# Turning normalized rows with scaled diagonal products, and letting the next product start block by block

## The chip, the cores and the metric

The kernel runs on one core of a Trainium2 chip. The metric is the device time of one execution of the whole program in microseconds (us). PE is TensorE, DVE VectorE, ACT ScalarE, POOL GpSimd and SP the engine whose queue issues the weight loads.

## The reference, cut to what matters

The reference is a small network: two layers of a first model, then one of a second, on 256 tokens (`SEQ`) of width 1024 (`D`), all in float32. Between the large parts stand norms over the width:

```python
def layer_norm(x, g, b):
    mu = jnp.mean(xf, axis=-1, keepdims=True)
    var = jnp.mean(jnp.square(xf - mu), axis=-1, keepdims=True)
    y = (xf - mu) * lax.rsqrt(var + LN_EPS) * g + b
...
h = rmsnorm(x, norm1_g) * (1.0 + sc1) + sh1      # second model, before its mixer
h2 = rmsnorm(x, norm2_g) * (1.0 + sc2) + sh2     # before its mixture of experts
return rmsnorm(x, final_norm_g)
```

The order is: mixer (attention and a state-space scan), norm, mixture of experts, norm, mLSTM mixer, norm, mixture, norm; then rms norm, three-branch mixer, rms norm, mixture with 32 experts, and the last rms norm.

## The kernel before, in words

The stream of tokens lies in `net.x` as two row tiles (i = 0, 1) of 128 tokens by 1024. Products want the tokens along the free axis, so each norm also makes `net.xT`, eight blocks (k = 0 to 7) of 128 features by 256 tokens. A phase is a class with one method per engine; each engine runs through the list `PHASES` in order, so the order on an engine is the order of the code, and engines meet at semaphores. DVE, ACT and POOL wait for each of their own instructions before the next (`Steps`, L71).

Seven norms lie in the list. ln0 and ln2 stand before the first two mixtures, ln1 before the mLSTM mixer, ln3 directly before rms0 (with nothing between), rms1 before the third mixture, and rms2 at the end. A turned norm (`LayerNorm` L389, `RmsNorm` L1489) runs like this for a row tile:

- DVE adds the last product to x (L496, L2779, L2368) and takes statistics (L401, L403, L404), or ACT sums squares (L1540, L1551) and DVE forms the mean (L1509, L1513, L1514).
- POOL raises the variance to the power -0.5 (L467, L1609).
- DVE writes the normalized rows, 128 by 1024, to scratch `xn` (L414, L1522).
- PE turns the eight blocks into two PSUM banks, four in each, by `pe.transpose` (L439, L1590).
- ACT evicts the first bank, blocks 0 to 3 (L478, L1563), and DVE the second, blocks 4 to 7 (L457, L1602), with the norm's gain and offset as per-partition scalars.

PE then waits until all four banks of the two row tiles are free (`wait_freed`, L114, called at L441 and L1592) before it goes on to the next phase's first product. That is the router's logits in a mixture (L2498), the gate strips in mLSTM and in the three-branch mixer (`small_strips`, L263). In the mixtures the scratch rows `xn` are also used later: `self.src` (L2455) is the same memory, and L2528 gathers tokens out of it. Between the logits and the gather lie one ACT copy (L2850), a fold on PE (L2505), zero products that open the output banks (L2509), and a chain of small DVE operations that picks experts and slots (L2696 to L2735).

ln3 is different: it isn't turned. DVE makes the finished rows in place (`finish`, L423 and L425, 128 by 1024 each), ACT squares the whole row (L1540), and rms0 normalizes and turns those.

POOL clears three buffers of a mixture (L2801, L2803) directly after the second `pow` of the norm before it. Before rms0 PE makes a row of gates (L1476); before the second row tile of rms1 it makes the strips for another (L1456).

## Time and profile before

| | us |
|---|---|
| median of 3 runs (1987.6 to 1993.73) | 1990.02 |
| the profiled execution, whole | 1990.63 |
| its span, first to last instruction | 1988.7 |
| PE busy | 1805.1 (91%) |
| DVE busy | 576.9 (29%) |
| ACT busy | 354.3 (18%) |
| POOL busy | 209.1 (11%) |

The rest of the page is an average over stages. The norms are short stretches in which PE isn't full; they are read from the timeline and the chain of waits. TensorE's granted clock is given as a share of its high level (2.4 GHz): 1.00 is the high and 0.50 the low level of 1.2 GHz. A float32 product stands as two MATMUL instructions; a transpose stands as one.

### The profile page before, as it was taken

The page shows a single profiled execution, that of the slowest core. Times are in us where ns is not written, and L with a number is a line of the kernel's source. Part 1 is how long each engine was busy: PE and PEld are TensorE (multiplying, and loading weights), DVE is VectorE, ACT ScalarE, POOL GpSimd, SP SyncE. Part 2 cuts the span into 40 slices and gives each one's busy share as a digit, 9 for nine tenths or more (in the row PEclk, how much of TensorE's full clock was granted, in tenths as well). Part 3 has the DMA queues.
Part 4 walks back from the last instruction along what each step waited for, and adds up shares of the span by engine and source line. Part 5 has one row for each costly group of instructions (what it writes and reads, how often), then busy time and mean ns, then how long its engine had stood idle before and what let it go on. Part 6 is the DMA issues. An engine that isn't in the chain of part 4 may idle for free.

```text
span 1988.7 us, 21335 instructions
## 1 busy us (share of the span) xinstructions
PE 1805.1 (91%) x6924; PEld 942.6 (47%) x6925; DVE 576.9 (29%) x1242; ACT 354.3 (18%) x654; POOL 209.1 (11%) x347
## 2 busy tenths in 40 slices
PE   8888699799978998999989999999988998888886
PEld 7444333485733336855865476444443333333332
DVE  8882400487641013321263321001131000000002
ACT  1242211212312112022141100112022111101101
POOL 0551122000002210000000000000001101101100
PEclk9868899898989998999999999999989999999999
DMA  9003399657325994323412334432255999999995
GB/s 367 22 1 146 138 382 397 248 222 285 145 110 229 393 397 188 140 116 136 180 75 95 148 136 160 162 133 95 121 239 206 422 422 422 422 422 422 422 422 237
DMA packets 70438, 468.81 MB, mean 236 GB/s; under 512 B 7848, under 2 KB 12112, under 8 KB 15072
## 3 DMA queue, kind: packets, MB, share of 16 engines
q1 hardware_dynamic: 66016, 457.56, 57.0%
q10 hardware_dynamic: 4352, 10.35, 1.5%
q8 instruction: 40, 0.66, 0.1%
q14 instruction: 30, 0.25, 0.0%
HBM read 466.82 MB, written 1.06 MB: 235 GB/s over the span
## 4 chain that ended last, share of the span: by engine, by line
PE 62%; DVE 16%; DMA 15%; issue 3%; ACT 2%; ACTq 1%; POOL 0%; SPq 0%; DVEq 0%; POOLq 0%
PE bank L238 17%; DMA ring_sb<-stream 15%; PE bank L2630 11%; PE bank L251 10%; PE bank L1628 4%; PE bank L2646 4%; PE bank L2670 4%; PE bank L2528 2%; DVE scratch_sb L1136 2%; DVE scratch_sb L1331 2%; DVE scratch_sb L997 2%; PE bank L916 1%; PE bank L1900 1%; PE bank L1272 1%; DVE scratch_sb L1419 1%
## 5 line engine op out<-in xcount | busy, mean ns | idle before, releaser
L2630 PE MATMUL bank<-ring_sb,scratch_sb 128*64 128x512 f32 x1536 | 344.2, 595 | 53.3 <-DMA ring_sb<-stream 29.3
L251 PE MATMUL bank<-xT_sb,ring_sb 128*128 128x256 f32 x1216 | 265.4, 381 | 0.0
L2630 PEld LDWEIGHTS bank<-ring_sb,scratch_sb 128*64 128x64 f32 x1536 | 116.8, 137 | 280.5 <-issue 280.5
L251 PEld LDWEIGHTS bank<-xT_sb,ring_sb 128*128 128x128 f32 x1216 | 231.5, 191 | 34.3 <-issue 2.9
L2670 PE MATMUL bank<-ring_sb,scratch_sb 128*64 128x512 f32 x768 | 171.9, 596 | 10.5 <-ACT scratch_sb L2889 10.5
L238 PE MATMUL bank<-ring_sb,xT_sb 128*128 128x512 f32 x416 | 179.3, 592 | 0.0
L238 PE MATMUL bank<-ring_sb,scratch_sb 128*128 128x512 f32 x384 | 170.5, 606 | 7.0 <-ACTq L2264 3.6
L2791 DVE TENSOR_TENSOR scratch_sb<-scratch_sb,bank 128x256 f32<-128x256 f32 (+1 forms) x32 | 17.7, 554 | 410.8 <-PE bank L2630 272.1
L238 PEld LDWEIGHTS bank<-ring_sb,xT_sb 128*128 128x128 f32 x416 | 79.0, 190 | 98.2 <-issue 98.1
L238 PEld LDWEIGHTS bank<-ring_sb,scratch_sb 128*128 128x128 f32 x384 | 74.2, 194 | 100.1 <-issue 92.0
L2646 PE MATMUL bank<-scratch_sb 128*128 128x512 f32 x256 | 118.4, 605 | 0.0
L2889 ACT ACTIVATE scratch_sb<-bank 128x256 f32<-128x256 f32 (+1 forms) x96 | 45.4, 490 | 400.9 <-PE bank L2654 255.1
L2796 DVE COPY scratch_sb<-bank 128x512 f32<-128x512 f32 x32 | 22.1, 692 | 300.3 <-PE bank L2670 300.3
L2670 PEld LDWEIGHTS bank<-ring_sb,scratch_sb 128*64 128x64 f32 x768 | 59.3, 137 | 101.3 <-issue 101.3
L2832 POOL COPY scratch_sb<-scratch_sb 128x512 f32 x64 | 37.3, 612 | 569.7 <-PEq L2549 537.0
L1628 PE MATMUL bank<-ring_sb,xT_sb 128*128 128x512 f32 x192 | 84.5, 592 | 0.0
L2646 PEld LDWEIGHTS bank<-scratch_sb 128*128 128x128 f32 x256 | 46.0, 189 | 71.9 <-issue 71.9
L2839 POOL TENSOR_SCALAR scratch_sb<-iota_sb,scratch_sb 128x64 f32<-128x64 f32 x128 | 72.1, 581 | 0.2
L1628 PEld LDWEIGHTS bank<-ring_sb,xT_sb 128*128 128x128 f32 x192 | 36.3, 190 | 42.0 <-issue 41.6
L2528 PE MATMUL bank<-scratch_sb 128*128 128x512 f32 x96 | 46.1, 639 | 10.9 <-DVEq L2737 10.8
L2892 ACT ACTIVATE scratch_sb<-bank 128x256 f32<-128x256 f32 (+1 forms) x32 | 15.7, 491 | 203.3 <-PE bank L2630 203.3
L1331 DVE SCALAR_TENSOR_TENSOR scratch_sb<-ring_sb,mod_sb,scratch_sb 128x512 f32<-128x512 f32 x56 | 42.1, 752 | 2.9 <-DVE scratch_sb L637 0.2
(405 smaller groups left out, 1738.1 us busy)
## 6 DMA issues: line engine op xcount, KB each, us to landing
ring_sb<-stream SPq DMA_DIRECT2D x432, 1024.0 KB, 10.3
rows_sb<-rows ACTq DMA_DIRECT2D x12, 512.0 KB, 4.7
xT_sb<-xT SPq DMA_DIRECT2D x2, 512.0 KB, 7.3
x_sb<-x SPq DMA_DIRECT2D x1, 1024.0 KB, 19.9
scratch_sb<-bias_by_distance ACTq DMA_DIRECT2D x1, 1024.0 KB, 5.2
out<-x_sb ACTq DMA_DIRECT2D x2, 512.0 KB, 2.6
scratch_sb<-decay ACTq DMA_DIRECT2D x1, 768.0 KB, 5.2
small_sb<-small SPq DMA_DIRECT2D x1, 640.0 KB, 13.6
```

Source lines behind the costliest of these rows:

```text
L238: mm = pe.matmul(t[:, :], actT[:, k, i * P:(i + 1) * P], w[:, k % 4, :], start=k == 0, stop=k == kt - 1)
L251: mm = pe.matmul(t[:, m * SEQ:(m + 1) * SEQ], w[:, k % 4, n0:n0 + P], actT[:, k, :], start=k == 0, stop=k == kt - 1)
L997: tt = lambda o, a, b, op: s(dve.tensor_tensor(o, a, b, op))
L1136: self.net.dv(dve.tensor_tensor_scan(xs, self.w[:, 3, j:j + 1].to_broadcast([P, SEQ]), xs, 0.0, ALU.mult, ALU.add))
L1331: net.dv(dve.scalar_tensor_tensor(part, w[:, k, :], c, part, ALU.mult, ALU.add))
L1628: mm = pe.matmul(self.gate_bank[:, :], net.xT[:, kk, i * P:(i + 1) * P], w[:, k, :], start=kk == 0, stop=kk == KT - 1)
L2528: mm = pe.matmul(t[:, :], self.src[:, i, k * P:(k + 1) * P], self.pick[i], start=i == 0, stop=i == 1)
L2630: mm = pe.matmul(t[e * TILE:(e + 1) * TILE, :], self.xs[e][:, kk, :], ws[e][:, k, :], start=kk == 0, stop=kk == KT - 1, skip_group_check=True)
L2646: pe.matmul(T.bank[2 * i + c][:, :], self.scatter[:, i * P:(i + 1) * P], self.y[:, c * 512:(c + 1) * 512], start=False, stop=False, skip_g ...
L2670: mm = pe.matmul(T.bank[6 + c][e * TILE:(e + 1) * TILE, :], self.hidT[:, ff, e * TILE:(e + 1) * TILE], ws[e][:, f, c * 512:(c + 1) * 512], ...
L2839: pool.tensor_scalar(self.weigh[:, i, e * TILE:(e + 1) * TILE], self.net.iota[:, tile * TILE:(tile + 1) * TILE], self.of_pair[:, 0, i, e:e ...
L2889: act.activation(out, src, ACT.Copy).then_inc(self.tile_sem(f"freed{b}", over), 1)
```

## The change

- **Layer norms ln0, ln1, ln2.** DVE no longer writes normalized rows. It writes two diagonals of 128 by 128 per row tile: minus the mean times the reciprocal deviation, and the reciprocal deviation. PE opens a bank with a product of ones and the first diagonal, spread four times over 512 columns, and adds on top of it, block by block, the product of x with the second diagonal. One small DVE operation is added to the statistics, and one after the diagonals.
- **rms0 and rms1.** One diagonal, one product a block, no ones product. The division by the width moves into the scale of ACT's square, and the two DVE operations of the mean become one. The same holds for the mean of rms2.
- **Waits.** `wait_freed` goes. Each eviction counts up a semaphore (`turned_low` by ACT, `turned_high` by DVE), and the next product waits before each of its eight blocks (`await_xT`). Evictions run in the order 0, 2, 1, 3 (0, 1, 2, 3 in rms1).
- **Rows for the gather.** ACT writes the normalized rows after the logits copy (`keep_rows`, two activations of 128 by 1024), and the gather waits for a second count of `logits_kept`.
- **ln3 and rms0.** The finish goes in halves of 512, ACT squares half rows, and row tile 0 gets its diagonal before row tile 1 is finished. The copies of the gate rows on ACT come after the evictions.
- Two semaphores of the mixers become shared with a base; one wait on `c_ready` goes.

```diff
+    def expect_xT(self, low):
+
+        order = {"low": low, "high": [k + 4 for k in low]}
+        for half, ks in order.items():
+            for pos, k in enumerate(ks):
+                self.xT_waits[k] = (self.sem(f"turned_{half}"), 8 * self.n_norms + 4 + pos + 1)
+        self.n_norms += 1
+        return self.n_norms - 1
+
+    def await_xT(self, pe, k):
+
+        if k in self.xT_waits:
+            sem, value = self.xT_waits.pop(k)
+            pe.wait_ge(sem, value)
...
@@ -403,24 +416,47 @@
             s(dve.bn_aggr(st[:, 32 + 4 * i:34 + 4 * i], st[:, 16 * i:16 * i + 12]))
             s(dve.tensor_scalar(st[:, 34 + 4 * i:35 + 4 * i], st[:, 33 + 4 * i:34 + 4 * i], LN_EPS, None, ALU.add))
             dve.sem_inc(self.s("var"), 1)
+            if self.n < 3:
+                s(dve.tensor_scalar(st[:, 50 + i:51 + i], st[:, 32 + 4 * i:33 + 4 * i], -1.0, None, ALU.mult))
 
...
-        else:
-            dve.wait_ge(self.s("rstd"), self.base("rstd") + i + 1)
-            s(dve.tensor_scalar(self.xn[:, i, :], net.x[:, i, :], st[:, 32 + 4 * i:33 + 4 * i],
-                                st[:, 35 + 4 * i:36 + 4 * i], ALU.subtract, ALU.mult))
+            self.scaled_only(dve, i)
+            self.finish_halves(dve, i)
+            return
+        dve.wait_ge(self.s("rstd"), self.base("rstd") + i + 1)
+        rstd, minus = st[:, 35 + 4 * i:36 + 4 * i], st[:, 50 + i:51 + i]
+        s(dve.tensor_scalar(self.diag[:, 2 * i, :], net.ident[:, :], minus, rstd, ALU.mult, ALU.mult))
+        s(dve.tensor_scalar(self.diag[:, 2 * i + 1, :], net.ident[:, :], rstd, None, ALU.mult))
         dve.sem_inc(self.s("normed"), 1)
-
-    def finish(self, dve, i):
+        s(dve.tensor_tensor(st[:, 52 + i:53 + i], minus, rstd, ALU.mult))
...
         for i in range(NT):
             pe.wait_ge(self.s("normed"), self.base("normed") + i + 1)
+            shift = self.diag[:, 2 * i, :].unsqueeze(1).to_broadcast([P, 4, P])
             for c in range(2):
                 t = net.T.open(pe, (self.tag, i, c))
+                pe.matmul(t[:, :].rearrange("p (k t) -> p k t", k=4), net.ones[:, 0:P], shift, start=True, stop=False,
+                          skip_group_check=True)
                 for k in range(4):
                     n0 = (4 * c + k) * P
-                    mm = pe.transpose(t[:, k * P:(k + 1) * P], self.xn[:, i, n0:n0 + P], net.ident[:, :])
+                    mm = pe.matmul(t[:, k * P:(k + 1) * P], net.x[:, i, n0:n0 + P], self.diag[:, 2 * i + 1, :],
+                                   start=False, stop=True, skip_group_check=True)
                 net.T.close((self.tag, i, c), mm)
-        net.T.wait_freed(pe, [(self.tag, i, c) for i in range(NT) for c in range(2)])
+        self.index = net.expect_xT(self.low)
...
     def vector(self, dve):
         net, s = self.net, self.net.dv
+        if self.n == 3:
+            self.following.mean(dve, 0)
+            self.scaled_only(dve, 1)
+            self.following.normalize(dve, 0)
+            self.finish_halves(dve, 1)
+            return
         self.normalize(dve, 1)
-        for i in range(NT if self.n < 3 else 0):
+        for i in range(NT):
             net.T.take(dve, (self.tag, i, 1))
-            for j in range(4, 8):
-                out, t, g, b = self.turned(i, 1, j)
+            for j in self.low:
+                out, t, g, b = self.turned(i, 1, 4 + j)
                 s(dve.tensor_scalar(out, t, g, b, ALU.mult, ALU.add))
+                dve.sem_inc(net.sem("turned_high"), 1)
             net.T.free(dve, (self.tag, i, 1))
...
         for i in range(NT):
             net.T.take(act, (self.tag, i, 0))
-            for j in range(4):
+            for j in self.low:
                 out, t, g, b = self.turned(i, 0, j)
                 net.ac(act.activation(out, t, ACT.Identity, scale=g, bias=b))
+                act.sem_inc(net.sem("turned_low"), 1)
             net.T.free(act, (self.tag, i, 0))
+
+    def keep_rows(self, act, out):
+
+        net, st = self.net, self.net.stat
+        net.T.take(act, (self.tag, NT - 1, 1))
+        act.wait_ge(net.sem("turned_high"), 8 * self.index + 1)
+        for i in range(NT):
+            net.ac(act.activation(out[:, i, :], net.x[:, i, :], ACT.Identity, scale=st[:, 35 + 4 * i:36 + 4 * i],
+                                  bias=st[:, 52 + i:53 + i]))
...
-        self.junk = Arena(net.scratch, JUNK).take(D)
+        self.shared = {"rms": {"mean": NT, "rstd": NT, "normed": NT, "squares": 2 * NT,
+                               "chunk_ready": 2 * NT if n else 0}}
+        self.diag = Arena(net.scratch, NORMED).take(NT * P, NT, P)
+        self.junk = Arena(net.scratch, JUNK).take(512)
         self.strips = Arena(net.scratch, JUNK + D).take(D)
+        self.low = ((0, 2, 1, 3), (0, 1, 2, 3), ())[n]
...
+    def mean(self, dve, i):
+
+        net, st = self.net, self.net.stat
+        dve.wait_ge(self.s("squares"), self.base("squares") + self.squares_at(i, 1))
+        a = 40 + 2 * i
+        net.dv(dve.tensor_scalar(st[:, 2 + i:3 + i], st[:, a:a + 1], st[:, a + 1:a + 2], RMS_EPS, ALU.add, ALU.add))
+        dve.sem_inc(self.s("mean"), 1)
+
     def normalize(self, dve, i):
         net, s, st = self.net, self.net.dv, self.net.stat
-        if self.n == 0:
-            dve.wait_ge(self.s("squares"), self.base("squares") + i + 1)
-            s(dve.tensor_scalar(st[:, 2 + i:3 + i], st[:, i:i + 1], 1.0 / D, RMS_EPS, ALU.mult, ALU.add))
-        else:
-            dve.wait_ge(self.s("squares"), self.base("squares") + self.squares_at(i, 1))
-            a = 40 + 2 * i
-            s(dve.tensor_tensor(st[:, i:i + 1], st[:, a:a + 1], st[:, a + 1:a + 2], ALU.add))
-            s(dve.tensor_scalar(st[:, 2 + i:3 + i], st[:, i:i + 1], 1.0 / D, RMS_EPS, ALU.mult, ALU.add))
-        dve.sem_inc(self.s("mean"), 1)
+        if self.n:
+            self.mean(dve, i)
         dve.wait_ge(self.s("rstd"), self.base("rstd") + i + 1)
         if self.n == 2:
             self.rows_here(dve)
             s(dve.scalar_tensor_tensor(net.x[:, i, :], net.x[:, i, :], st[:, 4 + i:5 + i], net.rows[:, 1, :], ALU.mult,
                                        ALU.mult))
         else:
-            s(dve.tensor_scalar(self.xn[:, i, :], net.x[:, i, :], st[:, 4 + i:5 + i], None, ALU.mult))
+            s(dve.tensor_scalar(self.diag[:, i, :], net.ident[:, :], st[:, 4 + i:5 + i], None, ALU.mult))
         dve.sem_inc(self.s("normed"), 1)
 
...
+        for n, (i, c) in enumerate(self.chunks()):
+            if self.n == 0:
+                act.wait_ge(ln.s("normed"), ln.base("normed") + n + 1)
+            else:
+                act.wait_ge(self.s("chunk_ready"), self.base("chunk_ready") + n + 1)
+            a = 40 + 2 * i + c
+            s(act.activation(self.junk, net.x[:, i, c * 512:(c + 1) * 512], ACT.Square, scale=D ** -0.5,
+                             accum_out=st[:, a:a + 1]))
+            act.sem_inc(self.s("squares"), 1)
...
                 t = net.T.open(pe, (self.tag, i, c))
                 for k in range(4):
                     n0 = (4 * c + k) * P
-                    mm = pe.transpose(t[:, k * P:(k + 1) * P], self.xn[:, i, n0:n0 + P], net.ident[:, :])
+                    mm = pe.matmul(t[:, k * P:(k + 1) * P], net.x[:, i, n0:n0 + P], self.diag[:, i, :], start=True,
+                                   stop=True)
                 net.T.close((self.tag, i, c), mm)
-        net.T.wait_freed(pe, [(self.tag, i, c) for i in range(NT) for c in range(2)])
+        self.index = net.expect_xT(self.low)
 
     def vector(self, dve):
         net, s = self.net, self.net.dv
-        for i in range(self.n > 0, NT):
-            self.normalize(dve, i)
-        for i in range(NT if self.n < 2 else 0):
+        if self.n == 2:
+            self.normalize(dve, 1)
+            return
+        if self.n == 1:
+            self.normalize(dve, 1)
+        for i in range(NT):
             net.T.take(dve, (self.tag, i, 1))
-            for j in range(4, 8):
-                out, t, scale, bias = self.turned(i, 1, j)
+            for j in self.low:
+                out, t, scale, bias = self.turned(i, 1, 4 + j)
                 s(dve.tensor_scalar(out, t, scale, bias, ALU.mult, ALU.add))
+                dve.sem_inc(net.sem("turned_high"), 1)
+                if (self.n, i, j) == (0, 0, 2):
+                    self.mean(dve, 1)
             net.T.free(dve, (self.tag, i, 1))
+            if (self.n, i) == (0, 0):
+                self.normalize(dve, 1)
...
+
+    def keep_rows(self, act, out):
+
+        net, st = self.net, self.net.stat
+        net.T.take(act, (self.tag, NT - 1, 1))
+        for i in range(NT):
+            net.ac(act.activation(out[:, i, :], net.x[:, i, :], ACT.Copy, scale=st[:, 4 + i:5 + i]))
...
         for j in range(per):
             for m in range(strips):
                 k = m * per + j
+                net.await_xT(pe, k)
                 mm = pe.matmul(t[m * width:(m + 1) * width, 0:SEQ], net.small[:, k, at:at + width], net.xT[:, k, :],
                                start=j == 0, stop=j == per - 1, skip_group_check=True)
...
+        pe.wait_ge(self.s("logits_kept"), base("logits_kept") + 2)
         pe.wait_ge(self.s("slots_ready"), base("slots_ready") + 1)
...
         t = T.take(act, (self.tag, "logits"))
         s(act.activation(self.logitsT, t[:, 0:SEQ], ACT.Copy))
         T.free(act, (self.tag, "logits"))
+        act.sem_inc(self.s("logits_kept"), 1)
+        self.prior.keep_rows(act, self.src)
         act.sem_inc(self.s("logits_kept"), 1)
```

In `small_strips` a line `self.await_xT(pe, k)` stands before each matmul as well, and `finish_halves` is the second operation of `finish` (L425) in two halves, each followed by a count of `normed`.

## Rows read from the trace of the kernel before

**Rows 1.** The page, chain that ended last, by engine: share of the span.

```profile
PE 62%; DVE 16%; DMA 15%; issue 3%; ACT 2%; ACTq 1%; POOL 0%; SPq 0%; DVEq 0%; POOLq 0%
```

**Rows 2.** Chain of waits in order of time, ln0: start us, us, what.

```profile
201.78 2.44 DVE scratch_sb L414
204.32 1.98 PE bank L439 x8
...
208.40 1.97 PE bank L2498 x16
210.39 0.39 ACT scratch_sb L2850
```

**Rows 3.** Timeline, ln0, POOL and DVE: start, us, engine, line, operation [idle before].

```profile
198.09 0.81 DVE L414 TENSOR_SCALAR scratch_sb<-x_sb,stat_sb 128x1024 f32<-128x1024 f32 x1 [0.78 <-POOLq L468]
...
201.85 1.81 POOL L2801 MEMSET scratch_sb<- 128x2048 f32 x1 [0.15 <-POOL stat_sb L467]
203.72 1.38 POOL L2803 MEMSET scratch_sb<- 128x1024 f32 x1
204.36 1.75 DVE L457 TENSOR_SCALAR xT_sb<-bank,cols_sb 128x128 f32<-128x128 f32 x4 [0.15 <-DVE scratch_sb L414]
```

**Rows 4.** Groups by line and shape: busy us, mean ns of one | idle before.

```profile
L637 DVE TENSOR_SCALAR scratch_sb<-scratch_sb 128x128 f32<-128x128 f32 x16 | 4.6, 286 | 0.6
L1540 ACT ACTIVATE scratch_sb<-x_sb 128x1024 f32<-128x1024 f32 x2 | 2.1, 1056 | 5.0 <-DVEq L416 5.0
```

**Rows 5.** Timeline of PE, dense stretches of one shape each.

```profile
185.64 13.04 PE L916 MATMUL bank<-ring_sb,scratch_sb 128*128 128x512 f32 x30
...
570.35 1.04 PE L439 MATMUL bank<-ident_sb,scratch_sb 128*128 128x128 f32 x8
...
1000.57 3.81 PE L1879 MATMUL bank<-scratch_sb 128*128 128x128 f32 x32 [0.85 <-issue]
```

**Rows 6.** Stretches of 1 us: length, PE busy (count), PEclk, DMA share, GB/s.

```profile
202.00:203.00 1.00, 0.00 (x0) 0.86 0.95 393
...
376.00:377.00 1.00, 1.00 (x8) 0.90 0.47 197
...
390.00:391.00 1.00, 1.00 (x5) 0.78 0.00 0
...
759.00:760.00 1.00, 0.41 (x3) 0.96 0.02 8
...
1475.00:1476.00 1.00, 0.00 (x0) 0.94 1.08 459
```

**Rows 7.** Timeline, ln1 and the start of mLSTM.

```profile
375.92 1.17 PE L439 MATMUL bank<-ident_sb,scratch_sb 128*128 128x128 f32 x8 [3.61 <-DVEq L416]
...
385.67 0.38 ACT L270 ACTIVATE scratch_sb<-bank 128x256 f32<-128x256 f32 x1 [2.65 <-PE bank L263]
```

**Rows 8.** Timeline, ln3 and rms0.

```profile
749.05 0.69 DVE L2779 SCALAR_TENSOR_TENSOR x_sb<-x_sb,bank 128x512 f32<-128x512 f32 x1 [0.15 <-DVE x_sb L425]
...
755.80 3.61 PE L1590 MATMUL bank<-ident_sb,scratch_sb 128*128 128x128 f32 x16 [4.76 <-DVEq L1523]
...
761.76 1.27 PE L263 MATMUL bank<-xT_sb,small_sb 128*32 128x256 f32 x16 [2.35 <-DVEq L111]
```

**Rows 9.** Timeline, rms1 to the logits of the third mixture.

```profile
1468.20 3.64 PE L1456 MATMUL bank<-ring_sb,mod_sb 128*32 128x512 f32 x32
...
1470.96 2.42 DVE L1522 TENSOR_SCALAR scratch_sb<-x_sb,stat_sb 128x1024 f32<-128x1024 f32 x1 [0.77 <-POOLq L1610]
...
1473.49 1.09 PE L1590 MATMUL bank<-ident_sb,scratch_sb 128*128 128x128 f32 x8 [1.66 <-DVEq L1523]
...
1477.49 3.68 PE L2498 MATMUL bank<-xT_sb,small_sb 128*64 128x256 f32 x16 [2.90 <-DVEq L111]
```

**Rows 10.** Timeline, ACT before the exponentials, and the mean of rms2.

```profile
217.71 0.30 ACT L2855 ACTIVATE scratch_sb<-scratch_sb 128x4 f32<-128x4 f32 x1 [5.48 <-DVEq L2719]
...
1983.19 0.16 DVE L1513 TENSOR_TENSOR stat_sb<-stat_sb 128x1 f32<-128x1 f32 x1 [0.99 <-ACTq L1553]
```

More of the change, by code:

```diff
@@ L111, in free @@
         eng.sem_inc(self.freed[self.jobs[key][0]], 1)
-    def wait_freed(self, eng, keys):
-        for b, k in (self.jobs[key] for key in keys):
-            eng.wait_ge(self.freed[b], k + 1)
 class Arena:
@@ L391 @@
     joins = False
-    shared = {"ln": {"var": NT, "rstd": NT, "normed": NT, "finished": 1}}
+    low = (0, 2, 1, 3)
     def __init__(self, net, n):
         self.net, self.n, self.tag = net, n, f"ln{n}"
-        self.xn = Arena(net.scratch, NORMED).take(NT * D, NT, D)
+        self.shared = {"ln": {"var": NT, "rstd": NT, "normed": NT if n < 3 else 2 * NT, "finished": 1}}
+        self.diag = Arena(net.scratch, NORMED).take(2 * NT * P, 2 * NT, P)
     def take_chunk(self, dve, i, c):
@@ L423, in finish, with finish_halves @@
         s(dve.scalar_tensor_tensor(x, x, st[:, 32 + 4 * i:33 + 4 * i], net.rows[:, 0, :], ALU.subtract, ALU.mult))
+    def finish_halves(self, dve, i):
+        net, s, st = self.net, self.net.dv, self.net.stat
+        dve.wait_ge(self.s("rstd"), self.base("rstd") + i + 1)
+        for c in range(2):
+            x = net.x[:, i, 512 * c:512 * c + 512]
+            s(dve.scalar_tensor_tensor(x, x, st[:, 35 + 4 * i:36 + 4 * i], net.rows[:, 1, 512 * c:512 * c + 512],
+                                       ALU.mult, ALU.add))
+            dve.sem_inc(self.s("normed"), 1)
+        if i == NT - 1:
+            dve.sem_inc(self.s("finished"), 1)
+    def finish(self, dve, i):
+        net, s, st = self.net, self.net.dv, self.net.stat
+        x = net.x[:, i, :]
+        self.scaled_only(dve, i)
         dve.wait_ge(self.s("rstd"), self.base("rstd") + i + 1)
@@ L698 @@
     tag = "fox"
-    shared = {"head": HEAD_COUNTS}
+    shared = {"head": HEAD_COUNTS, "forget": {"f_ready": 1, "log_ready": 1}}
     INPUT, STATE, REST = (0, 1), (2, 3), (4, 5, 6, 7)
@@ L1171 @@
     tag = "mlstm"
-    shared = {"head": HEAD_COUNTS}
+    shared = {"head": HEAD_COUNTS, "forget": {"f_ready": 1, "log_ready": 1}}
     mlstm = True
@@ L1534, in scalar @@
         net, s, st = self.net, self.net.ac, self.net.stat
+        ln = self.prior
         if self.n == 0:
[L1536 removed]
             keep_gate_strips(net, act, "gt1", self.strips)
[L1538 to L1548 removed]
+        for n, (i, c) in enumerate(self.chunks()):
+            if self.n == 0:
+                act.wait_ge(ln.s("normed"), ln.base("normed") + n + 1)
+            else:
                 act.wait_ge(self.s("chunk_ready"), self.base("chunk_ready") + n + 1)
[L1550 to L1553 removed]
+            a = 40 + 2 * i + c
+            s(act.activation(self.junk, net.x[:, i, c * 512:(c + 1) * 512], ACT.Square, scale=D ** -0.5,
+                             accum_out=st[:, a:a + 1]))
+            act.sem_inc(self.s("squares"), 1)
         if self.n == 2:
@@ L1560, in scalar @@
             net.T.take(act, (self.tag, i, 0))
-            for j in range(4):
+            for j in self.low:
                 out, t, scale, bias = self.turned(i, 0, j)
                 s(act.activation(out, t, ACT.Identity, scale=scale, bias=bias))
+                act.sem_inc(net.sem("turned_low"), 1)
             net.T.free(act, (self.tag, i, 0))
@@ L1566, in scalar @@
                 keep_gate_strips(net, act, "gt2", self.following.gt)
+        if self.n == 0:
+            act.wait_ge(ln.s("finished"), ln.base("finished") + 1)
+            for c in range(2):
+                t = net.T.take(act, ("gt1", c))
+                s(act.activation(net.rows[:, 1, c * 512:(c + 1) * 512], t[:, :], ACT.Copy, scale=1.0 / 32))
+                net.T.free(act, ("gt1", c))
     def turned(self, i, c, j):
```

34 lines of the change are left out of this document (7 added, 27 removed).

## The prediction

> **What bounds the kernel now.** I read the chain that ended last first [rows 1]: PE holds 62% of it, DVE 16%, DMA 15%. So over most of the span a norm matters only by how long it keeps PE from its next product, and I read each norm in the chain of waits and then in the timeline. In ln0 [rows 2] the chain runs from POOL to DVE's normalized rows at 201.78, to the second row tile's transposes at 204.32, through DVE's evictions, to the logits at 208.40, and to ACT at 210.39. The reader is to see that nothing else runs beside it: from PE's start on row tile 1 to ACT's copy it is 6.07 us. ln2 has the same pattern, 376 us later. The 1 us stretches [rows 6] show what PE's clock does there: it fell to the low level at 202.9, after a burst of 1.1 us and a pause, at 376.9 in the burst after a pause, and at 1475.9.
>
> A shift of PE's start behind a norm passes on to the end whole, in either direction: the products behind it keep PE full. In the third mixture, where DMA paces, I take the same, since the loads had stopped before the first expert started and restart with PE; the bound if not is a loss of the rms1 gain below.
>
> **Prices.** A 128x512 float32 product costs 13.04/30 x 2 = 0.87 us at the high level; a 128x128 one 3.81/32 x 2 = 0.24; a transpose 1.04/8 = 0.13 [rows 5]. At the low level I double them: eight transposes took 1.97 there [rows 2] against 1.04. So a row tile of a layer norm goes from 1.04 to 2 x (0.87 + 4 x 0.24) = 3.65 us (low: 1.97 to 7.3), and one of an rms norm to 8 x 0.24 = 1.9 (low 3.8).
> A diagonal on DVE: the same operation and size takes 0.29 [rows 4], about 0.35 for the one with two scalars. The pair with its gap is 0.67, against 0.81 for the full rows [rows 3]. Where no other engine interferes this gives back 0.14, less 0.2 for the small operation behind it.
> An eviction paces at 1.75/4 = 0.45 [rows 3].
> The waits removed: before, DVE's last eviction ended at 204.36 + 2 x 1.75 + 0.2 = 208.1 [rows 3], and ACT's copy came at 210.39, 2.3 us later. After, only the last block's product stays, about a quarter of 1.97 with its start: 0.6. So from row tile 1's start to ACT's copy it is 3.65 + 4 x 0.45 + 0.6 = 6.05 with the clock high, 9.7 low, against 6.07. **The ones product and the dearer turns eat up all of the block-by-block start even at the high clock.**
>
> **POOL's memsets.** In ln0 L414 took 2.44 [rows 2] where the first took 0.81 [rows 3]: the memset of 2048 columns lay beside it, and L414 ended 0.54 after it. So DVE stood still until 203.66. The same is in ln2 and in rms1 (2.42, [rows 9]). A diagonal stands still as well: the first of a pair is done at 203.75; by then the second memset (1.38, of which some 0.5 was its own wait) is next and the second diagonal comes at about 204.7. PE starts at 204.85 instead of 204.32, +0.55. Other end: the diagonals slip in before the memset, PE is ready when row tile 0 is done, 198.85 + 3.65 = 202.5: -1.8. I take +0.55, as all three cases in the trace stood still.
> The Trainium skill, SBUF — State Buffer, "Who interferes with whom", says that whoever issues first gets the shared ports for the whole instruction. In the trace DVE's operation is stamped 0.07 us before the memset [rows 2, 3] and lost all the same, so here the trace speaks against the rule; by the rule the sum would be 2 x 2.35 us lower.
>
> **ln0 and ln2.** Before, PE began row tile 0 at 198.09 + 0.81 + 0.1 = 199.0 [rows 3] and paused from 200.1 to 204.32, 4.2 us; now the pause is 2.4 (202.5 to 204.85). Nearest rows: after a pause of 1.66 in rms1 the clock was still high, and it fell at 1475.9, after that row tile [rows 6, 9]; after 4.2 it was low. I take a fall part of the way through row tile 1. Bounds +0.5 (high) and +4.2 (low); value +2.0 each, +4.0 for both. keep_rows costs nothing: 2 x 1.06 [rows 4] lies in ACT's 5.48 us of idle before the exponentials [rows 10]; without this cover it would be 2.1. The gather's new wait has nothing queued behind it but the gather, and comes 10 us later than the rows.
>
> **ln1.** No memset. The clock falls at 376.9 [rows 6] during row tile 0, which PE starts at 375.75 [rows 7]. 1.15 us done, 2.5 left, which takes 3.5 us low and the rest high (in rms0 PE began low at 755.80 and the clock was high again at 759.0 [rows 6, 8]): 381.1. Row tile 1, ready since 379.4, now queues behind it: 384.8, evictions and last block 387.2, against 385.67 [rows 7]: +1.5. DVE's four finishes (5.3 us) move with it, still under the first product. Then a gain: before, PE stayed low until 390.2 [rows 6]; some 4 us of work after 386.2 could run up to 2.0 faster, since PE has now just worked 9 us. I take -0.5 of that: +1.0. Bounds -2.2 (all high) and +3.4 (all low).
>
> **ln3 and rms0.** Row tile 0 gets its diagonal before row tile 1's finish: x at 749.74 [rows 8], statistics 1.2, mean 0.2, one finish half-pair 1.3, diagonal 0.3, and 0.15 for halves: PE starts at 753.1 instead of 755.80. But row tile 1 now waits for more. Its mean stands behind two evictions of row tile 0's second bank: with the clock low that bank is ready at 756.9, two evictions 757.8, mean and POOL 758.65, diagonal 759.0, PE 762.9, evictions and last block 765.3, against 761.76 + 1.27 = 763.03: +2.2. With the clock high: bank 755.0, diagonal 757.2, PE 759.2, evictions and last block 761.4: -1.6. Before, PE began its 16 transposes low (3.61 us, [rows 8]) after a pause of 4.76; the pause is now about 2.1, so it is unsure at which level it starts. I take +0.5, a little above the middle. The gate-row copies (1.3 us on ACT) move behind the evictions; their banks are wanted only by the third bank from there, 6 us later.
>
> **rms1.** One diagonal, so only the first memset holds it: 1472.75 against 1473.38. One mean operation fewer is inside that. PE runs row tile 0 (1.9), the gate strips (3.64, [rows 9]) and row tile 1 from 1472.9 without a pause, so the clock stays high: bank at 1474.8, evictions 1476.6, last block 1477.0, against 1477.49 + 3.68 = 1481.2: -4.2. If the product runs low it paces itself: 1475.3 + 3.7 = 1479.0, -2.2. I take -3.7.
>
> **rms2.** One 0.16 operation with its gap fewer on each row tile [rows 10], both on the chain: -0.35.
>
> **Sum.** +4.0 + 1.0 + 0.5 - 3.7 - 0.35 = +1.45 us. Against the profiled execution's own time, 1990.63 (its span is 1988.7), this is 1992.1; that execution lies 0.6 above the median of the runs, so I predict **1991.5**.
>
> **Rivals.**
> - *PE stays warm.* PE has two to three times the turning work and shorter pauses, so every norm runs at the high level: 2 x 0.5 - 2.2 - 1.6 - 4.2 - 0.35 = -7.35, that is 1982.7. For it: rms1's pause of 1.66. Against it: the pauses left are 2.4 in ln0 and ln2, and ln1 and rms0 begin after pauses in which the clock had fallen. The Trainium skill, TensorE: Matmul & The Clock Gate, "Part 1: The HAM clock gate", says that the throttled state is the default and activity releases it, which is this case; at 376.9 the trace shows a fall in the middle of work, so the rule alone doesn't decide it.
> - *The diagonals pass before the memset*, with my clock: 1.45 - 2 x 2.35 = -3.25, 1986.8; with a warm PE too, -12, 1978.
> - *The ones product at a low clock*, the case on the other side: in ln0 and ln2 PE falls to the low level as row tile 1 starts, and 5.4 us of extra matmul time stands where 1.7 of waits went. It decides from the point where row tile 1 takes over 3.65 + 1.6 us. Bounds: 2 x 4.2 + 3.4 + 2.2 - 2.2 - 0.35 = +11.45, 2001.5; a typical one, ln0 and ln2 alone low, +5.9, 1996.
>
> **How the numbers follow.** Forecast 0.48 (its own range 1986 to 1996), warm PE 0.22, diagonals first 0.12, low clock 0.18. The range takes in most of the rivals: 1983 to 1999. A change below 0.3%, 6 us, is what a measurement of this kernel can't tell from none. Faster by over that (below 1984.0): most of the warm case and some of diagonals first, 0.24. Slower (above 1996.0): most of the low-clock case and a little of the forecast, 0.18. Within: 0.58.
>
> **What would show it.** From the second row tile's first product to ACT's logits copy in ln0: about 8 us if I am right, 6 if PE stays high, 9.7 if low. L414's successors in ln0: the second diagonal ending near 204.7, or both before 202.5. In rms1 the logits end 3.7 us closer to the last product of the mixer. PEclk in the stretch of row tile 1. I am wrong if the products after a norm don't start at the shifted time, or if a stretch without norms changes its length by over 2 us.

## The result, and the profile after

The changed kernel takes **1.0034 of the time of the kernel before (95% interval 1.0021 to 1.0046)**, 6.8 us more on 1990; the medians of 13 runs each are 2001.03 and 1991.57 us. The quotient of the medians is 1.0048: the runs of the kernel before spread from 1987.60 to 2001.25, those of the changed kernel from 1998.52 to 2003.59, so the median of the kernel before is the less steady number. The profiled execution took 2002.07 (span 2000.3). The predicted 1991.5 is 5 us short of 1990 x 1.0034 = 1996.8. That lies inside the stated range of 1983 to 1999, but just above the forecast's own 1986 to 1996, and in the class "slower", to which I gave 0.18.

The page of the changed kernel, chain that ended last, by engine; it answers to [rows 1]:

```profile
PE 64%; DMA 15%; DVE 13%; issue 4%; ACT 2%; ACTq 1%; POOL 0%; SPq 0%; DVEq 0%; POOLq 0%
```

PE's share grew and DVE's shrank: work moved from DVE to PE, the engine that already held the chain.

ln0 of the changed kernel, timeline: start, us, engine, line, operation [idle before]. It answers to [rows 2, 3].

```profile
205.12 1.81 POOL L2874 MEMSET scratch_sb<- 128x2048 f32 x1 [0.15 <-POOL stat_sb L514]
205.13 1.88 DVE L431 TENSOR_SCALAR scratch_sb<-ident_sb,stat_sb 128x128 f32<-128x128 f32 x1 [0.55 <-POOLq L515]
206.99 0.95 POOL L2876 MEMSET scratch_sb<- 128x1024 f32 x1
207.04 0.97 DVE L432 TENSOR_SCALAR scratch_sb<-ident_sb,stat_sb 128x128 f32<-128x128 f32 x1
...
208.13 1.12 PE L474 MATMUL bank<-scratch_sb,ones_sb 128*128 128x512 f32 x2 [2.27 <-DVEq L433]
...
211.83 2.93 PE L2570 MATMUL bank<-xT_sb,small_sb 128*32 128x256 f32 x16
...
214.80 0.38 ACT L2923 ACTIVATE scratch_sb<-bank 128x256 f32<-128x256 f32 x1 [2.43 <-PE bank L2570]
```

The second row tile's two diagonals stand still beside POOL's two memsets. From its first product to ACT's copy it is 214.80 - 208.13 = 6.67 us, and row tile 1 is turned in 211.83 - 208.13 = 3.70.

rms0, timelines of PE and DVE (the same columns), to set against [rows 8]:

```profile
759.69 1.28 DVE L441 SCALAR_TENSOR_TENSOR x_sb<-x_sb,stat_sb,rows_sb 128x1024 f32<-128x1024 f32 x1
760.04 1.34 POOL L1673 TENSOR_TENSOR stat_sb<-stat_sb 128x1 f32<-128x1 f32 x1 [0.18 <-POOL stat_sb L514]
...
761.94 3.79 PE L1645 MATMUL bank<-scratch_sb,x_sb 128*128 128x128 f32 x16 [2.73 <-DVEq L1578]
...
766.33 0.41 DVE L1661 TENSOR_SCALAR xT_sb<-bank,mod_sb 128x128 f32<-128x128 f32 x1 [0.15 <-DVE xT_sb L1661]
766.89 0.21 DVE L1564 TENSOR_SCALAR stat_sb<-stat_sb 128x1 f32<-128x1 f32 x1 [0.15 <-DVE xT_sb L1661]
...
768.47 0.28 DVE L1577 TENSOR_SCALAR scratch_sb<-ident_sb,stat_sb 128x128 f32<-128x128 f32 x1 [0.24 <-DVE xT_sb L1661]
...
768.86 3.78 PE L1645 MATMUL bank<-scratch_sb,x_sb 128*128 128x128 f32 x16 [3.14 <-DVEq L1578]
...
772.58 2.93 PE L275 MATMUL bank<-xT_sb,small_sb 128*32 128x256 f32 x16
```

The products behind rms0, L275, end at 775.51 where the same ones of before ended at 763.03 [rows 8].

The second row tile's mean waits behind two evictions, and PE pauses 3.14 us for its diagonal. Both row tiles run at the low clock (3.79 us for 16), as the window shows for the second: length, busy and count of PE, PEld, DVE, ACT, POOL, then PEclk, DMA share, GB/s.

```profile
768.00:772.00 4.00, 3.14 (x14) 3.14 (x15) 0.51 (x2) 0.90 (x2) 0.00 (x0) 0.50 0.00 0
```

rms1, chain of waits of the changed kernel, to set against [rows 9]:

```profile
1487.97 0.42 DVE xT_sb L1661
...
1488.51 0.03 DVEq L111
1488.54 0.04 issue
1488.59 1.97 PE bank L2570 x16
1490.58 0.39 ACT scratch_sb L2923
```

All sixteen logits products start after DVE's last eviction. The releaser is L111, the freeing of a bank, and not L1662, the count of a block: the block-by-block start doesn't happen here.

The stages, worked out from the start of one operation at each stage's end (the first statistics L401 before a layer norm, DVE's read of the route bank L2696 behind ln0, ln2 and rms1, the last conv copy L1409 behind ln1, the later products of the projection L1725 behind rms0, DVE's last addition to x L2368 before rms1, ACT's first copy of gathered tokens L2865 behind the third routing; lines of before), as the change in the stage's length against the first profile of before (us). "b2" is a second profile of the kernel before, "a1" and "a2" two of the changed kernel, the others are the experiments below:

```
            b2     a1     a2     x1     x2     x3     x4     x5     x6     x7     x9    x10    x12
Fox       +3.1   +3.1   +1.4   +0.8   +1.6   +1.5   +1.4   -1.1   +0.8   +3.0   +1.4   +1.3   +0.5
ln0        0.0   +0.9   +2.5   -1.3   -1.3   +2.5   +0.8    0.0   -1.4   -1.3   -2.9   -1.4   -2.3
moe0      +3.7   +2.6   +3.8   +1.5   +1.6   +1.3   +1.0   +2.5   +2.2   +1.6   +1.6   +3.9   +1.5
ln1       +0.7   +1.0   +0.8   -2.0   -2.0   +0.1   +0.1   -2.3   +0.9   -2.6   -2.5   +1.1   -2.5
mLSTM     +0.1   -0.1   -0.3   -0.3   -0.3   -3.3   -3.4   -0.3   -0.3   +0.3   +0.3    0.0   -0.1
ln2        0.0   +0.8   +0.8   -0.4   -0.4   +2.5   +2.5   +1.7   -1.4   -0.8   -2.9   -1.4   -1.9
moe1      +0.6   -0.5   -0.5   +0.4   +0.4   +2.8   +2.7   +0.8   +3.6   +3.2   -0.3   +3.5   +0.7
ln3+rms0   0.0   +3.2   +3.2   +3.6   -1.5   +3.2   -0.5   +3.2   +2.7   -1.5   -1.5   -1.2   -0.5
attention  0.0    0.0    0.0    0.0   -1.9   -1.9   +1.5   -1.9   -1.2   -1.1   -1.9   -0.8   +1.5
rms1       0.0   -2.1   -2.1   -2.1   +0.7   -3.5   -2.1   -2.1   -2.6   -3.5   -3.5   -3.5   -3.3
routing 3  0.0   +0.7   +0.8   +2.8    0.0   +2.6   +0.7   +2.7   +2.5    0.0   +0.1    0.0    0.0
moe2      +0.4   +2.2   +3.8   +0.6   +2.2   +3.4   +4.0   +0.5   +0.1   +0.1   +0.4   +0.2   -0.8
rms2       0.0   -0.3   -0.3   -0.3    0.0   -0.3   -0.3   -0.3   -0.3   -0.3   -0.3   -0.3   -0.3
```

Fox is the first mixer, moe0 to moe2 are the expert loops. The Fox row is the measure of chance: its code is the same in all columns, and it spans -1.1 to +3.1. The rows of rms0 and rms1 repeat far better; ln0 of the changed kernel stands at +0.9 or +2.5. A row of a norm reaches some way into the products behind it, so it holds also what these gained or lost by TensorE's clock.

### The profile page after: what moved, and what is told of

It is laid out like the page before. It is cut to its first block, busy times and chain, and to the rows that moved or that the text cites. A ratio compares the mean times of both kernels' runs of the same rounds, so it can differ in the third digit from the quotient of the medians.

```text
span 2000.3 us, 21664 instructions
## 1 busy us (share of the span) xinstructions
PE 1830.1 (91%) x7028; PEld 957.8 (48%) x7029; DVE 576.3 (29%) x1258; ACT 362.0 (18%) x664; POOL 207.9 (10%) x347
## 4 chain that ended last, share of the span: by engine, by line
PE 64%; DMA 15%; DVE 13%; issue 4%; ACT 2%; ACTq 1%; POOL 0%; SPq 0%; DVEq 0%; POOLq 0%
PE bank L249 17%; DMA ring_sb<-stream 15%; PE bank L2703 11%; PE bank L262 10%; PE bank L1699 4%; PE bank L2719 4%; PE bank L2743 4%; PE bank L2601 2%; DVE scratch_sb L1388 2%; DVE scratch_sb L1054 2%; PE bank L973 1%; DVE scratch_sb L1193 1%; PE bank L1971 1%; PE bank L1329 1%; DVE scratch_sb L1475 1%
```

## The experiments

Ratios are to the kernel before; x11 and x13 are single runs. The difference of two such ratios is known to about 0.0017, which is 3.4 us. The edits are shown shortened.

**x1_ln_old.** LayerNorm back to transposes.

```
- shift = diag[2i].to_broadcast(4 blocks); pe.matmul(t, ones, shift, start=True, stop=False)
- mm = pe.matmul(t[block], net.x[:, i, n0:n0 + P], self.diag[:, 2 * i + 1, :], start=False, ...)
+ mm = pe.transpose(t[block], self.xn[:, i, n0:n0 + P], net.ident[:, :])
```

> The changed kernel with ln0 to ln2 turned the old way (normalized 128x1024 rows written by DVE, 16 transposes, no ones product, no diagonals, rows already kept for the gather); the waits block by block and the three RMS parts stay changed. Theory A (the norms themselves cost: of the 6.8 us, by the shifts between the two traces, ln0 has +0.85, ln1 +1.5, ln2 +0.25, rms0 +3.2, rms1 -2.1): 2 to 4 us come back, since the waits taken away keep their gain, so 1.001 to 1.0025 of the kernel before. Theory B (most of the loss lies outside the norms, in the Fox mixer (+3.1) and the expert loops (+2 each), where the code is the same, set by when TensorE's clock falls): the time changes by chance, anything from 1.000 to 1.005, and the shift at ln0's start differs from +3.1 while the Fox code is untouched. Theory C (the LayerNorm part is the whole loss): 1.000 or below.

Measured 1.0003 (0.9991 to 1.0014): 6 us back, more than A's 4. C wanted 1.000 or below, and the interval doesn't exclude it. ln0 goes from +0.9 or +2.5 to -1.3, ln1 from +0.9 to -2.0. By this run the diagonals of the layer norms cost about as much as the whole change loses, and what the rest wins and loses about cancels.

**x2_waits_only.** The kernel before with `await_xT` in place of `wait_freed`, and with the evictions in the new order.

> The kernel before with one part of the change alone: the next product waits for each turned block by itself (and the blocks are evicted in the order 0, 2, 1, 3) in place of a wait for all four banks. Theory A: the wait is the gain of the change. In the traces PE's first strip product came 1.7 us earlier against the last eviction at ln0; at ln1, ln2 and rms0 about 1 us each; nothing at rms1, where the logits bank is the one DVE is still evicting. Sum -3 to -5 us: 0.9975 to 0.9985 of before. Theory B (PE's clock and the later chain take it back, the logits' own end depends only on the last block): -0.5 us or less, 0.9995 to 1.001.

Measured 0.9985 (0.9976 to 0.9995): A, at its upper end. Every row of a norm but rms1 gets shorter (-1.3, -2.0, -0.4, -1.5). Most of that is not the wait itself: counted to ACT's copy of the logits or strips the four are -0.8, -0.3, -0.4 and +0.3, and the rest came in the products behind. Of the change's parts it is the only one that was tried by itself and won.

**x3_bank.** The logits of the second and third mixture in another bank.

```
- t = T.open(pe, (self.tag, "logits"), free)
+ t = T.open(pe, (self.tag, "logits"), ((7,), (4,), (7,))[self.n])
```

> The changed kernel with the logits of the second and third mixture put in another PSUM bank (4 and 7 for 6 and 5). Theory A: in the changed kernel the third mixture's logits could not start block by block, since their bank is that of the last turned tile: the 16 products began at 1488.59, 0.21 us after DVE's last eviction at 1488.38. In another bank they start when the first blocks are there, 14 of 16 products are done by the last eviction, and rms1 ends 1.0 to 1.6 us earlier; the second mixture's bank is freed by ACT at about the time of the last block, gain 0 to 0.3 us. 0.9992 to 0.9995 of the changed kernel, so 1.0025 to 1.003 of before. Theory B (the wait was for the block itself, not for the bank): the products start where they did, and the time is the changed kernel's, 1.0034.

Measured 1.0032 (1.0021 to 1.0043). The mechanism is A's; the time can't decide, since the interval holds both. Timeline of x3_bank, rms1 to the routing:

```profile
1483.65 0.65 PE L2570 MATMUL bank<-xT_sb,small_sb 128*64 128x256 f32 x2
...
1484.58 2.33 PE L2570 MATMUL bank<-xT_sb,small_sb 128*64 128x256 f32 x14 [0.28 <-DVEq L1662]
...
1485.60 0.94 ACTq L333 DMA_DIRECT2D rows_sb<-rows  x2
...
1485.74 0.41 DVE L1661 TENSOR_SCALAR xT_sb<-bank,mod_sb 128x128 f32<-128x128 f32 x1 [0.15 <-DVE xT_sb L1661]
...
1496.51 0.22 DVE L2798 TENSOR_TENSOR_SCAN scratch_sb<-ones_sb,bank 128x32 f32<-128x32 f32 x1 [2.46 <-DMA rows_sb<-rows]
```

The products now start before DVE's last eviction and wait for L1662, the block; rms1 gains 1.4 more. But then DVE's scan stands 2.46 us for the rows that ACT issued after its evictions, and the routing of the third mixture gives it all back (+2.6 against +0.7). The bank isn't the only way to this wait: in x1 and x5, with the old bank and rms1 at -2.1, the scan stands 2.23 and 2.24 us for the same rows, and their routing is at +2.8 and +2.7.

**x4_rms0_order.** rms0's second mean and diagonal ahead of DVE's evictions of row tile 0.

```
+ if self.n == 0: self.mean(dve, 1)
+ self.normalize(dve, 1)
  for i in range(NT): ... evictions ...
-     if (self.n, i, j) == (0, 0, 2): self.mean(dve, 1)
- if (self.n, i) == (0, 0): self.normalize(dve, 1)
```

> The changed kernel with the second row tile's mean and diagonal of rms0 made ahead of DVE's evictions of the first row tile, as before, not between and behind them. Theory A: rms0 lost 3.2 us since this mean waited behind two evictions (766.89), its diagonal came at 768.47 and the second row tile's products at 768.86; put ahead, the mean can run at about 765.2 when its squares are done and the second row tile starts 1.0 to 2.0 us earlier, worth 1 to 2 us: 1.0025 to 1.003 of before. Theory B: what rms0 lost is TensorE's low clock (16 products in 3.79 us for each row tile between 761.9 and 772.7, as against 1.0 to 2.0 us high): the second row tile is behind the first on PE in any case, which ends at 765.7, so at most 0.5 to 1 us is gained, and DVE's four evictions of row tile 0, now later, take it back: 1.0034 within 0.0005.

Measured 1.0004 (0.9993 to 1.0014), twice what A allowed. PE and DVE in rms0:

```profile
759.18 3.78 PE L1645 MATMUL bank<-scratch_sb,x_sb 128*128 128x128 f32 x16 [2.73 <-DVEq L1578]
...
761.76 0.21 DVE L1564 TENSOR_SCALAR stat_sb<-stat_sb 128x1 f32<-128x1 f32 x1 [0.89 <-ACTq L1601]
...
762.74 0.29 DVE L1577 TENSOR_SCALAR scratch_sb<-ident_sb,stat_sb 128x128 f32<-128x128 f32 x1 [0.77 <-POOLq L1671]
...
763.14 3.05 PE L1645 MATMUL bank<-scratch_sb,x_sb 128*128 128x128 f32 x16 [0.18 <-DVEq L1578]
763.18 0.41 DVE L1662 TENSOR_SCALAR xT_sb<-bank,mod_sb 128x128 f32<-128x128 f32 x1 [0.15 <-DVE scratch_sb L1577]
```

PE's pause shrinks from 3.14 us to 0.18, and the second row tile begins 3.96 us behind the first in place of 6.92. The gain is 3.0 of pause and 0.7 of clock: the second row tile took 3.05 in place of 3.78, the clock having come back in the middle of it. DVE's first eviction starts beside row tile 1's products and costs nothing. In the norm this is 3.7 us of the 6 measured; the rest lies in rows that chance moves.

**x5_no_ones.** Leaves out the shift by the mean.

```
- pe.matmul(t, net.ones[:, 0:P], shift, start=True, stop=False, skip_group_check=True)
```

> The changed kernel without the ones product of ln0 to ln2 (it leaves out the shift by the mean; both diagonals are still made). In the runs so far the three LayerNorms turned by diagonals cost 6 us more than turned by transposes (1.0034 against 1.0003), by the shifts within each norm +2.1 to +3.8 us at ln0, +3 at ln1, +1.2 to +2.8 at ln2. Theory A (TensorE's extra work is the price): the ones product took 1.1 us high for four (0.27 us each) and 2.08 us low for the first two of ln1; without it the first row tile is turned 0.3 to 1.0 us sooner and the last by as much again, so ln0 to ln2 give back 3 to 4 us: 1.0015 to 1.002. Theory B (DVE's two diagonals and POOL's memset beside them are the price, 1.88 and 0.97 us): the ones product hides behind the eviction pace, 1 us comes back at most: 1.003 or more.

Measured 1.0003 (0.9990 to 1.0016), beyond A. ln1, which has no memset, goes from +0.9 to -2.3, as with transposes (-2.0): there the ones product is all of the price. ln0 goes from +0.9 or +2.5 to 0.0. ln2 doesn't gain: it is at +1.7, with the ones product at +0.8 or +2.5, so no price can be read there.

**x6_memset_late.** `pool.wait_ge(prior normed, both row tiles)` ahead of POOL's memsets.

> The changed kernel with POOL's memsets of ln0, ln2 and rms1's following mixture behind a wait for the norm's second diagonal. Theory B: the diagonals take 0.25 to 0.35 us each in place of 1.88 and 0.97 (ln0) and 1.97 (rms1), so the last row tile's turn starts 1.5 to 2.3 us earlier at each of the three: 4 to 6 us, 1.0005 to 1.0015 of before. Theory A (the port is held by something else, or the memset only moves onto DVE's evictions or the routing operations behind them): diagonals short, but the blank tiles and the evictions later by as much: under 1.5 us, 1.0027 or more.

Measured 1.0013 (1.0004 to 1.0022): B. Timeline of ln0:

```profile
202.75 0.35 DVE L431 TENSOR_SCALAR scratch_sb<-ident_sb,stat_sb 128x128 f32<-128x128 f32 x1 [0.55 <-POOLq L515]
203.13 0.28 DVE L432 TENSOR_SCALAR scratch_sb<-ident_sb,stat_sb 128x128 f32<-128x128 f32 x1
203.52 0.30 PEld L474 LDWEIGHTS bank<-scratch_sb,ones_sb 128*128 128x128 f32 x2 [0.24 <-DVEq L433]
...
203.53 1.81 POOL L2875 MEMSET scratch_sb<- 128x2048 f32 x1 [0.95 <-DVEq L433]
203.76 0.41 DVE L503 TENSOR_SCALAR xT_sb<-bank,cols_sb 128x128 f32<-128x128 f32 x1
```

The diagonals take 0.35 and 0.28 (1.88 and 0.97 in the changed kernel), and the memset beside the evictions costs them nothing: 0.41 as ever. ln0 and ln2 gain 2.2 to 3.9 us each against the changed kernel. At rms1 it is only 0.5, since PE is busy with the gate strips until then.

**x7_best and x9_best_memset.** x2 plus the bank of x3, rms1 (alone) turned by its diagonal, and ACT's loads for the third mixture ahead of its evictions; x9 adds the wait of x6.

```
+ if self.n == 1: self.following.early_loads(act)   # before, and both rows
  for i in range(NT): net.T.take(act, (self.tag, i, 0)) ...
```

> Built from the kernel before: its transposes in ln0 to ln2 and rms0, the waits block by block, rms1 alone turned by a diagonal with its rows kept behind the logits, the logits' banks changed, one operation for the mean in rms1 and rms2, and the loads of the third mixture's rows issued from ACT's queue ahead of its evictions in rms1 (with the bank changed, DVE's scan waited 2.46 us for these rows at 1496.5 while its inputs were there). Theory A: the parts add: waits -3 us (0.9985 measured), rms1 by diagonal -2.1 against +0.7 with the old turn, bank -1.4, rows -1.5 kept: -6 to -8.5 us, 0.9957 to 0.997. Theory B (what is won at rms1 is given back at the next gather or in the expert loop by TensorE's clock): -3 to -4 us, 0.998 to 0.9985.

> The kernel of x7_best with POOL's memsets in ln0, ln2 and rms1 behind a wait for the second row tile's normed flag. Theory A: at ln0 and ln2 DVE's write of the normalized rows (128x1024, 2.44 us beside the memset) falls to about 1.1 us, at rms1 the diagonal from 1.97 to about 0.3: 1.3 to 1.6 us each, 4 us in all, 0.002 below x7_best. Theory B (DVE's write itself is the limit, and a memset now beside the evictions holds them): the same as x7_best within 0.0007.

Measured **0.9963 (0.9948 to 0.9977)** and **0.9919 (0.9905 to 0.9933)**, 1978.37 us: A for both, the second twice as much as expected. x9 beats both kernels. With the rows early the routing stands at 0.0 and the expert loop at +0.1 to +0.4. Timeline of x9_best_memset, ln0:

```profile
203.17 0.81 DVE L431 TENSOR_SCALAR scratch_sb<-x_sb,stat_sb 128x1024 f32<-128x1024 f32 x1 [0.78 <-POOLq L486]
204.09 1.95 PE L456 MATMUL bank<-ident_sb,scratch_sb 128*128 128x128 f32 x8 [2.60 <-DVEq L433]
204.09 1.81 POOL L2838 MEMSET scratch_sb<- 128x2048 f32 x1 [1.01 <-DVEq L433]
```

The full normalized row takes 0.81 where it took 2.44 [rows 2]. Of the 8.8 us between x7 and x9, ln0 and ln2 show 3.7; the rest lies in unchanged stretches (moe1 3.5, Fox 1.6). In moe1 it goes with the clock: the low level took 17.1 us of that stage in x7 and 6.8 in x9.

**x10_repaired** (the changed kernel with x3, x4, x6 and the early loads) **and x12_repaired_no_ones** (the same without the ones product).

> The changed kernel with all four repairs together (rms0's second mean and diagonal ahead of the evictions; memsets behind the second diagonal; the logits' banks; the third mixture's rows loaded ahead of the evictions); all norms by diagonals, the ones product kept. From the shifts of the single repairs: rms0 -3.7, memset -2.2 to -3.9 at ln0 and ln2, bank and rows at rms1 -1.4 and -2.5, from +6.8: about -5 us, 0.9965 to 0.9985 of before. Against x9_best_memset (0.9919), which has the same repairs and the old turn in ln0 to ln2 and rms0: theory A (the ones product and the second diagonal are dearer than the row writes they replace) says 5 to 9 us slower, 0.996 to 0.999; theory B (once the memset is out of the way the diagonals are as good) within 2 us of it, 0.992 to 0.993.

> The repaired kernel (x10_repaired, 0.999) without the ones product of ln0 to ln2; it leaves out the shift by the mean. Theory A (the ones product is what keeps the diagonals behind the transposes): most of the 14 us between x10_repaired (0.999) and x9_best_memset (0.9919) goes, so 0.993 to 0.996. Theory B (the second diagonal, the rows kept behind the logits and the chance of the clock make the gap): 0.997 or more.

Measured 0.9990 (0.9976 to 1.0004) and 0.9945 (0.9928 to 0.9962): A in both, though x10 gained less than its repairs promised one by one. Even where the memsets' stall is gone the kernel without the ones product is 9 us faster. The profiles show 0.9, 3.6 and 0.5 of it in the three norms, and 5.2 in moe0 and moe1 behind them; rms0 and the attention, which it doesn't touch, go 3.0 the other way. So 5 us is the price that can be pointed at. x12 leaves out the shift and the ones product and is still 5 us behind x9, which turns with transposes.

**x11_after_again and x13_before_again.** Second profiles.

> The changed kernel once more, unchanged, for a second profile. If the +3.1 us at ln0's start, in code that the change does not touch, were the change's doing, it is there again; if it is where TensorE's clock fell in that execution, the shift here differs by more than 1 us, as in the other kernels so far (-1.1 to +3.0), and the norms' own shifts (ln0 +0.8 to +2.5, rms0 +3.2, rms1 -2.1) repeat.

> The kernel before once more, unchanged, for a second profile. If the profile of before that the shifts are counted from was typical, the stages with no change in them (Fox, the three expert loops, the attention) repeat within 0.5 us; if it was a lucky one for TensorE's clock, they come 1 to 3 us later here, and by as much the changed kernel's loss in these stages is no loss of the change.

x11: 2004.49 us; Fox +1.4 in place of +3.1, while rms0 (+3.2) and rms1 (-2.1) repeat to 0.01 us. x13: 1999.19 us, 8.5 later than the first profile of before, of it 3.1 in Fox, 3.7 in moe0, 0.7 in ln1 and 0.6 in moe1. The two lie on either side of what the kernel before does (medians of 1991.6 to 1996.0): stages outside the norms in a1 that are late by as much can't be called a loss of the change. In ln0 of a1 and a2 DVE and POOL take the same times, and the clock differs (ln0 starts 1.7 us earlier in a2); windows of a1 and then of a2 (columns as above):

```profile
208.00:212.00 4.00, 3.87 (x22) 2.77 (x24) 1.88 (x7) 1.46 (x4) 0.31 (x1) 1.00 1.01 420
```

```profile
208.00:212.00 4.00, 4.00 (x19) 2.73 (x17) 0.97 (x3) 1.83 (x4) 0.00 (x0) 0.61 1.02 422
```

## Why the prediction was right, and where it was not

- **Turns, evictions and removed waits in ln0 and ln2: right.** A row tile took 3.70 us high for my 3.65. The forecast of +2.0 each was a mean between clocks, counted to ACT's copy. Counted there it is +1.3 and +2.9 at ln0 (a1, a2) and +1.2 twice at ln2. By the rows the profiles that have this part as the change made it show +0.9, +2.5, +2.5, +0.8 at ln0 (a1, a2, x3, x4) and +0.8, +0.8, +2.5 at ln2 (a1, a2, x4), 1.7 and 1.3 in the mean. "8 us from first product to ACT's copy" was 6.67 in a1, where PEclk stayed at 1.00. The evictions pace at 0.56 each with the count behind them, not 0.45.
- **Memset: right.** I had the first diagonal done at 203.75 and the second 0.95 later. In a1, where the memset starts 3.27 later, they end at 207.01 and 208.01, 1.00 apart. What I did not weigh is what x6 shows: the stall as a whole is worth 2.2 to 3.9 us at each of ln0 and ln2 in the changed kernel, and 1.6 and 2.1 with the old turn (x9 against x7).
- **ln1: right in the sum, by luck.** +1.0 forecast; +1.0 and +0.8 measured in a1 and a2 (+0.1 in x3 and x4). But I had it as +1.5 up to ACT's copy and -0.5 behind it. The copy of a1 came at 395.42, with the first statistics at 377.17 against 370.59 and the copy at 385.67 before [rows 7]: +3.2, and 2.1 came back behind it, where the clock was high again. PE was low from the start of row tile 0 (2.08 us for one ones product), not from its middle. x2 and x5 show what is inside the row: -2.0 with the waits alone, 2.4 to 3.3 for the ones product.

```profile
382.54 2.08 PE L474 MATMUL bank<-scratch_sb,ones_sb 128*128 128x512 f32 x2 [4.02 <-DVEq L433]
...
395.42 0.38 ACT L282 ACTIVATE scratch_sb<-bank 128x256 f32<-128x256 f32 x1 [2.10 <-PE bank L275]
```

- **ln3 and rms0: the step that failed.** I took +0.5 "a little above the middle" of -1.6 and +2.2; it was above my bound. At the place of the forecast, the end of the strips' products, it is +4.7 in a1 (775.51 against 763.03, with the first statistics at 749.70 against 741.89); 1.4 came back in the projection behind, where the clock was high and before had been low, which leaves the row at +3.2. The low clock held for both row tiles, which was the +2.2 case: the pause did not shorten to 2.1 but was 2.73. A row tile took 3.79 us low, as priced. Row tile 0 started 1.7 us earlier than before in place of 2.7. Of this 1.0, about 0.4 is POOL: its power took 1.34 us in place of 0.55, beside DVE's scaled rows (L441), and DVE stood 0.57 for it, where it stands 0.15 between two evictions; 0.36 is x itself, which came later by that much. x4 shows that the order was the choice that cost: 3.7 us.
- **rms1: the size wrong, the mechanism half there.** -3.7 forecast, -2.1 measured. The clock stayed high, as I had it, but the block-by-block start that I counted was shut off by the bank: the logits open the bank of the last turned tile. With another bank it is -3.5 (x3), which the routing behind it took back there.
- **rms2: right**, -0.27 for -0.35.
- **What stood in no term: the third mixture.** I took the rms1 gain to pass on to the end whole. Routing and expert loop gave back 2.9 and 4.6 us in a1 and a2. Of the kernels with waits block by block, all eight profiles with the loads late lose 2.2 to 6.0 there (x1 to x6, a1, a2; x2, whose rms1 isn't shorter, the least); the four with the loads early lie between -0.8 and +0.5. The early loads weren't tried alone: these four have the other bank too, so that they are the cause is likely but not shown. PEclk shows part of it: the stretch around the gather and the first experts, a1, then the same stretch of x7 (columns as above).

```profile
1510.00:1530.00 20.00, 16.81 (x53) 6.24 (x53) 0.00 (x0) 5.95 (x7) 3.72 (x8) 0.91 0.09 29
```

```profile
1498.00:1518.00 20.00, 16.81 (x61) 6.41 (x61) 0.00 (x0) 5.92 (x8) 3.72 (x8) 1.00 0.21 76
```

In the means over these profiles the norms' rows give 1.7 + 0.5 + 1.3 + 3.2 - 2.1 - 0.3 = +4.3 us against my +1.45, and the third mixture adds 3 to 5; the clock in mLSTM took up to 3.4 back in two of them. This comes near the 6.8, but a sum of single profiles to 1 us is more than the Fox row allows. x1, x4 and x5 each give back 6 of the 6.8 and x6 gives 4, so these can't be shares of one sum: the rows inside the norms are the safer prices. moe0 and moe1 don't follow the length of ln0 and ln2. They go with the time for which their stage had the low clock: in moe1 that was 6.8 us in a1, a2 and x9 (-0.3 to -0.5), 17.1 in x6, x7 and x10 (+3.2 to +3.6); in moe0 7.7 in the first profile of before, 16.2 in b2 (+3.7) and 17.1 in x10 (+3.9). What sets that time stays open.

By my own sign of being wrong, a stretch without norms that changes by over 2 us, I was wrong in a1: Fox +3.1, moe0 +2.6, moe2 +2.2. For Fox and moe0 b2 shows as much in an unchanged kernel (+3.1, +3.7), so that sign was too narrow. For moe2 it shows +0.4.

Three readings of mine were off, and nothing rests on them: ln2's stall lies 371.5 us behind ln0's, not 376; and the clock changed at 202.7, 376.8 and 390.4, not 202.9, 376.9 and 390.2, since a low stretch counts 0.50 in the mean and not 0.

Of the rivals, the ones product at a low clock (1996 typical) comes nearest in the number, not in the mechanism: it wanted ln0 and ln2 low, and in a1 both ran high; it was rms0 that ran low from end to end. A warm PE held in ln0, ln2 and rms1 of a1, not in ln1 and rms0, and in a2 not in ln0 either. So it was luck, and the width of the range, that the total lay inside: by the rows rms0 was missed by 2.7 us, rms1 by 1.6 and the third mixture, for which the sum had no term, by 3 to 5.

## What to carry to other kernels

Before moving work from an engine with slack to the one that holds the chain, price each wait around it by itself: here the fine-grained waits (0.9985), a memset moved by one wait, loads issued ahead of a few evictions and another bank, with a diagonal in rms1 alone and one operation fewer for the mean, were worth 16 us together. A block-by-block start needs its output bank free as well as its inputs, and an operation slipped in between evictions costs what the other engine then waits. Where the same program's profiles differ by 8 us, compare by stage, and take a second profile of the kernel before.
